# Paged K/V cache pages laid out with two tokens per partition, in a hybrid decoder step

## The reference, cut to what matters

```python
PAST_LEN = 2048; PAGE_SIZE = 128; MOBA_BLOCK = 256; MOBA_TOPK = 3     # 8 heads x 64
page_sum = sum(cache_k[layer, page_table], axis=token)                # per page, then two pages per block
gate = einsum('bthd,bnhd->bthn', q, kmean)                            # q . mean key of each block
_, sel = top_k(gate, 3)
s = einsum('bthd,bthnd->bthn', q, k_g) / sqrt(64) - slope * (t - pos) # ALiBi: needs each token's position
p = softmax(where(valid, s, -inf));  out = einsum('bthn,bthnd->bthd', p, v_g)
```

## Time and profile before

| | |
|---|---|
| median of 3 runs | 447.73 us (446.93 to 448.33) |
| profiled execution, first to last instruction (its span) | 446.5 us |
| instructions | 8259 |
| TensorE matmul busy | 416.1 us, 93% of the span |
| VectorE busy | 296.0 us, 66% |
| ScalarE busy | 181.6 us, 41% |
| GpSimd busy | 104.4 us, 23% |
| DMA | 109515 packets, 124.85 MB, mean 280 GB/s |
| cache pages | 128 loads of keys, 128 of values, 256 KB each |
| chain that ended last, by engine | PE 55%, DVE 18%, SPq 11%, issue 6%, DMA 5% |

### The profile page before, as it was taken

The page is one execution under the profiler, slowest core; times in us unless marked ns, Lnnn a source line. Parts: engine busy times, 40 slices in busy tenths (PEclk is TensorE's granted clock), DMA queues, the critical chain, the costliest instruction groups (busy, mean ns, idle before and its releaser), DMA issues.

```text
span 446.5 us, 8259 instructions
## 1 busy us (share of the span) xinstructions
PE 416.1 (93%) x2911; PEld 341.0 (76%) x2911; DVE 296.0 (66%) x383; ACT 181.6 (41%) x694; POOL 104.4 (23%) x133
## 2 busy tenths in 40 slices
PE   4999999999999998999798989999999999999990
PEld 4588887876866774664364369999999999999990
DVE  0496999999799976944351264766666877534536
ACT  1476568653377334011110043455554456224201
POOL 1003033995255231100000436211222221000002
PEclk9999999999999999999999999999999999999997
DMA  8999999999999999999999953566666685968002
GB/s 294 385 329 386 385 388 379 370 357 390 398 386 372 351 393 387 386 386 386 386 377 386 304 166 111 159 178 189 189 182 170 166 215 155 234 174 212 24 1 97
DMA packets 109515, 124.85 MB, mean 280 GB/s; under 512 B 5775, under 2 KB 66920, under 8 KB 109466
## 3 DMA queue, kind: packets, MB, share of 16 engines
q1 hardware_dynamic: 101138, 107.55, 72.5%
q10 hardware_dynamic: 8336, 16.78, 10.5%
HBM read 121.90 MB, written 2.61 MB: 279 GB/s over the span
## 4 chain that ended last, share of the span: by engine, by line
PE 55%; DVE 18%; SPq 11%; issue 6%; DMA 5%; POOL 2%; ACT 1%; DVEq 0%; POOLq 0%; ACTq 0%
PE ps L1815 11%; PE ps L1816 11%; PE ps L1817 11%; SPq L354 8%; DVE qk L930 5%; DVE T L940 5%; PE ps L1432 4%; PE ps L1627 4%; PE ps L1708 3%; PE ps L1603 3%; PE ps L1629 3%; PE ps L1372 3%; DMA wring<-in_cache_v 2%; DMA KV<-in_cache_k 2%; POOL x1l L605 1%
## 5 line engine op out<-in xcount | busy, mean ns | idle before, releaser
L1177 DVE TENSOR_TENSOR wlo<-KV,whi 128x2048 fp32r<-128x2048 f32 (+1 forms) x24 | 61.8, 2576 | 57.1 <-ACT whi L832 29.1
L1432 PE MATMUL ps<-xT,wring 128*128 128x264 f32 x384 | 89.6, 389 | 0.0
L1432 PEld LDWEIGHTS ps<-xT,wring 128*128 128x128 f32 x384 | 71.9, 191 | 13.4 <-issue 1.7
L1815 PE MATMUL ps<-x1h,whi 128*128 128x264 f32 x256 | 73.8, 288 | 0.2
L930 DVE TENSOR_TENSOR qk<-KV,qk 128x1536 f32<-128x1536 f32 (+1 forms) x32 | 67.8, 2122 | 9.2 <-DMA KV<-in_cache_k 5.5
L1817 PE MATMUL ps<-x1h,wlo 128*128 128x264 f32 x256 | 72.7, 284 | 0.0
L1816 PE MATMUL ps<-x1l,whi 128*128 128x264 f32 x256 | 72.7, 284 | 0.0
L662 ACT ACTIVATE qk<-qk 128x64 f32<-128x64 f32 x216 | 51.8, 244 | 28.5 <-POOL qk L553 21.1
L940 DVE TENSOR_REDUCE T<-qk 128x24 f32<-128x1536 f32 (+1 forms) x32 | 58.4, 1827 | 0.0
L1815 PE MATMUL ps<-fh,whi 128*128 128x264 f32 x176 | 50.4, 286 | 0.1
L1816 PE MATMUL ps<-fl,whi 128*128 128x264 f32 x176 | 50.0, 284 | 0.0
(11 more groups left out here) (218 smaller groups left out, 578.9 us busy)
## 6 DMA issues: line engine op xcount, KB each, us to landing
KV<-in_cache_k SPq DMA_DIRECT2D x128, 256.0 KB, 7.3
KV<-in_w_ffn_up SPq DMA_DIRECT2D x32, 512.0 KB, 5.1
KV<-in_cache_v SPq DMA_DIRECT2D x60, 256.0 KB, 8.5
wring<-in_cache_v SPq DMA_DIRECT2D x56, 256.0 KB, 7.5
KV<-in_w_ffn_down SPq DMA_DIRECT2D x8, 1408.0 KB, 7.0
wring<-in_w_in ACTq DMA_DIRECT2D x5, 2048.0 KB, 15.1
zbuf<-in_cache_v SPq DMA_DIRECT2D x12, 256.0 KB, 6.0
zbuf<-in_w_ffn_up SPq DMA_DIRECT2D x3, 1024.0 KB, 11.5
```

The lines of the kernel that those rows point to most:

```text
L1177: nc.vector.tensor_tensor(wlo[s][:, 0:n], w2[s][:, 0:n], whi[s][:, 0:n], ALU.subtract).then_inc(s_lo, 1)
L1432: ins = nc.tensor.matmul(ps[:, z_bank(n), 0:R], tile[k], xT[:, k, :], start=k == 0, stop=k == KT - 1)
L1815: nc.tensor.matmul(out, wh[k], xh[k], start=k == 0, stop=False)
```

## The change

The load of a page takes 64 partitions instead of 128, and two consecutive tokens per partition: page g of a slot goes to the partitions of the parity of g, and its tokens 2i and 2i + 1 lie side by side in the places of the two pages g - g % 2 and g - g % 2 + 1. In memory and in a partition's row these are 4 KB in one piece. Place (partition p, page place g) now holds token (p // 2) * 2 + g % 2 of page g - g % 2 + p % 2, and the constant c_bias is made by that rule. Nothing else is changed.

```diff
             def load(pages, ids, dst, landed):
                 for g in range(GP):
-                    sp.dma_start(dst[:, g, :], pages[bass.ds(ids[g], 1)].rearrange("o t d -> (o t) d")).then_inc(landed, 16)
+                    sp.dma_start(dst[g % 2:P:2, g - g % 2:g - g % 2 + 2, :],
+                                 pages[bass.ds(ids[g], 1)].rearrange("o (t j) d -> (o t) j d", j=2)).then_inc(landed, 16)
...
     tok = np.arange(P)
-    past = PAST - (np.arange(NPAGE)[None, :] * PAGE + tok[:, None])
+    g = np.arange(NPAGE)[None, :]
+    past = PAST - ((g - g % 2 + tok[:, None] % 2) * PAGE + tok[:, None] // 2 * 2 + g % 2)
```

## The result

The changed kernel is slower: 452.59 us (median of 7 runs, 449.60 to 453.36) against 448.33 beside it, a ratio of 1.0072 with a 95% interval of 1.0040 to 1.0103. Measured twice more on other occasions it had 450.39 us (1.0061, 1.0041 to 1.0081) and 449.87 us (1.0060, 1.0042 to 1.0077). So it costs 2 to 4 us. The forecast was 443.5 us, its range 441.0 to 450.0.

What follows compares the result with a forecast made beforehand. Full DMA engines bound the kernel to about 255 us, compute setting the pace at 140 to 155; TensorE's 6.7 us of late transfer waits were the ceiling. 447.7 - 5.1 (cheaper packets) + 0.9 (weights' stall) = 443.5 us, range 441.0 to 450.0.

Steps and rivals of the forecast that it cites:

- The term that I set to zero: SyncE's issue of the 256 page loads: any change in its time from half as many descriptors, taken as zero.
- Saved time before 155 us is lost: DMA time saved early gains nothing: at 140 to 155 us key loads wait for slots that VectorE and GpSimd free.
- The price of a packet: Cache page loads: one 4 KB packet takes 165 ns, two of 2 KB 176 to 178; 11 ns saved per pair.
- The destination's rival: Page loads writing every second partition: engines collide in SBUF, 4 KB packets take 195 ns, 465 us; chance 0.22.
- The weights' turn: w_in beside 4 KB key pages gets one third of the bytes; chunk 3.2 us later, TensorE stalls 1.8 us.
- +0.9: Net loss at the z tiles: half of the 1.8 us TensorE stall counted; ends 0 and 3.6 us.
- The rival with three late chunks: Three w_in chunks beside key loads are late: 7.2 us of stalls against 5.1 gained, 449.8 us; chance 0.08.
- -5.1: Late page loads, 155 to 252 us: cheaper packets shorten TensorE's waits by 5.1 us, under a 6.7 us ceiling.
- The rigid part: Everything after 252 us, behind the last value page, moves along unchanged with the shift before it.

Runs made afterwards that it cites:

- The halves: Against the kernel before, only keys or only values loaded in the new form: keys alone 450.37 us (1.0053), values alone 447.34 us (0.9989).

## Why the prediction was wrong

**The step that failed**: "SyncE is held up by full rings there, not by its own work, so I take zero." Its first part was true of the kernel before on the whole, and the row it was read from was the right one, but that row says "part of the time": half of the issues into wring and the key slots took the shortest time, 333 or 334 ns. What was left out is how near SyncE was to its own limit. The row had it: 333 ns to issue, some 2.1 us for a group, so that SyncE could feed about 1.05 MB in 2.1 us and 1.0 us of page numbers in every four groups, 4.19 MB in 9.4 us or 446 GB/s, against 389 drawn. That is a margin of 15%. The term that I set to zero measured 142 ns for each load, 112 x 0.142 = 15.9 us of SyncE's time in a stage of 90 us, and turned the margin into a lack, 361 against the 407 that the engines drew from 200 to 215 us. The range had no bound for it on the side of a loss, though the text itself said that the trace doesn't show this cost. The destination had no row either and got a rival with a price; this unknown got a value, and neither a range nor a rival.

**Saved time before 155 us is lost**: right, but for another reason from 128 us on. It is SyncE's pace, more than the slots, that leaves the queue short there (0.93 and 334 GB/s after, 0.99 and 347 before), and it is short to 175 us and later, where I had counted the engines as full.

**The price of a packet**: right. The 165 ns of a 4 KB packet at 200 to 215 us (worked out above) are the 165 that were taken. Where SyncE kept up the rate was 400 to 409 GB/s, as forecast. The destination's rival (465 us) fell with these two numbers and with the 92 ns of 2 KB packets into every second partition.

**The weights' turn**: the mechanism, the place and the wait were right, 1.94 us at the ninth z tile against 1.8, and a landing after 17.7 us against 14.8 + 3.2 - 0.4 = 17.6. The size was not: I counted half of it as given back and ended at +0.9 us. The clock that fell to 0.51 behind the wait, which the sum did not have, added 1.7 us, 1.5 came back, and 2.3 us stayed up to 112 us. What of that reaches the end is not settled: keys alone in the new form, which have this stall, lost 2.2 us in the timed runs (450.37 - 448.18), but 0.9 us in the profile, and without page numbers the changed kernel has the stall and loses nothing. The rival with three late chunks did not happen, there was one.

**The sum**: forecast -5.1 and +0.9. In the first profile +2.3 up to 112 us, and +2.6 behind it, where -5.1 was to be; in the third, where the rate held, the late stage gave back 3.5 us, after TensorE had fallen 4.5 us behind. The halves' losses, +2.2 us of the keys and -0.5 of the values, give 1.7 of the 2.0 to 4.3 us that the whole change lost; the remainder may be the hole, which showed only with both halves, and the scatter; that is argued, not shown.

**The rigid part** behind 252 us was right to 0.1 us.

What stays open: why the wait for ScalarE at 70 us is 1.8 to 1.9 us in some executions and 1.0 in others, with a drop of the clock behind it in some; how much of the scatter between executions of one kernel such drops are (at 176 to 178 us the clock was 1.00 in the first profile of the changed kernel and 0.50 in the other two); and why SyncE reaches value group 19 at 204.5 us in one execution and at 208.0 in another. Splitting the issue between two queues without changing the order of landing was not achieved, so that way to get the gain is not refuted.

## What to carry to other kernels

When a change alters the shape of a DMA, work out the issuing engine's own budget first: its time for each load, its other instructions between loads, and the bytes for each, as a rate beside the one that the engines draw. An engine that stands at full rings has a margin, and the margin is a number. Where the trace has no row for the new shape's issue, it needs a range on both sides and not a zero. And larger packets on one queue take bytes from the other (1.45 against 0.92 MB here, 1.15 each before): look for the transfer with the least slack on the other queue before the gain is counted, and count what a stand of TensorE costs in clock behind it.

## What the runs showed of the hardware

The time to issue a load of 256 KB from SyncE went with its shape: 333 ns for 128 rows of 2 KB, 468 ns for 64 rows of 4 KB on adjacent partitions, 475 ns for the same on every second, 604 ns for 64 rows in two pieces of 2 KB. Half as many rows were dearer to issue, which I had not reckoned with.

With the same 4 KB packets, 64 adjacent partitions in turns gave 265 GB/s and every second partition 408, from 200 to 215 us; 2 KB packets to all 128 gave 386.

The w_in chunk of 128 x 8 rows of 2 KB landed after 14.8 us beside page loads in 2 KB packets, and after 17.7 to 18.1 us beside 4 KB ones (17.7, 17.8 and 18.0 in the three profiles of the changed kernel, 18.1 with the keys alone in the new form).

A stand of TensorE of 1.94 us was followed by a granted clock of 0.51 and 0.63 in the next two stretches of 2 us; one of 2.24 us in another execution of the same kernel was not, and the same 16 matmuls took 5.49 us in the one and 3.80 in the other. Executions of one kernel differ by 1.7 us for such a place.
